# One decoder layer on one core: the sample maximum by way of TensorE, key sums one at a time, and low weights split on VectorE

## The reference

```python
z = x @ w_in                                  # q, k, v, u, two gates
s = einsum('bqhjd,bkhjd->bhjqk', q, k) * HEAD_DIM**-0.5 + bias   # 8 heads, two maps j
p = softmax(s); p_diff = p[:, :, 0] - lam * p[:, :, 1]
attn = rms_norm(einsum('bhqk,bkhe->bqhe', p_diff, v), subln_g) * (1 - lam_init)
ssm = g * sigmoid(g @ w_glu), g = gelu(s5_scan(u))               # 64 groups, 64 states
merged = sigmoid(gate_a) * (attn @ w_proj_attn) + sigmoid(gate_s) * (ssm @ w_proj_ssm)
h = layer_norm(alpha * x + merged @ w_out)
y = layer_norm(alpha * h + (silu(gate) * val) @ w_down)          # gate, val: conv(h @ w_up)
```

## Time and profile before

| | |
|---|---|
| runs, median | 1962.67 us (1961.89 to 1966.1, 3 runs) |
| profiled execution: time, span | 1960.97 us, 1959.1 us |
| mean granted clock of TensorE | 0.936 |
| PE matmul, busy | 1791.6 us (91%) |
| DVE, ACT, POOL busy | 1110.0, 604.7, 1116.0 us |
| DMA | 393.44 MB, 201 GB/s over the span |
| GpSimd line 620 (low weights), 166 instructions | 750.5 us |
| GpSimd line 583 (key products), 128 instructions | 299.2 us |
| VectorE line 1615 (key sums), 128 instructions | 153.9 us |

### The profile page before, as it was taken

How to read it: one execution, slowest core, us unless ns; L and a number is a source line. 1 busy time by engine, 2 the same in 40 slices (tenths; PEclk the granted TensorE clock), 3 DMA queues, 4 the chain that set the end, 5 groups by cost and what they waited for, 6 DMA issues and landing times.

```text
span 1959.1 us, 32040 instructions
## 1 busy us (share of the span) xinstructions
PE 1791.6 (91%) x11898; PEld 1530.8 (78%) x11898; DVE 1110.0 (57%) x1360; ACT 604.7 (31%) x927; POOL 1116.0 (57%) x383
## 2 busy tenths in 40 slices
PE   7899998898988969967999799999999997999997
PEld 5787665565655636646999799999999997999995
DVE  1353656556565563345950389999999999000004
ACT  2021222232222320212322354444444443333333
POOL 1036455465554643004777457777777777677771
PEclk9999898898988978978999989999999999999997
DMA  9766897888989866655656436666666665666651
GB/s 213 180 202 221 282 337 246 297 298 272 322 275 310 288 213 231 196 173 136 180 164 173 129 100 181 174 173 173 172 173 172 173 173 141 171 174 176 175 149 45
DMA packets 537197, 393.44 MB, mean 201 GB/s; under 512 B 23618, under 2 KB 502743, under 8 KB 536535
## 3 DMA queue, kind: packets, MB, share of 16 engines
q1 hardware_dynamic: 404944, 325.07, 55.4%
q10 hardware_dynamic: 132160, 67.11, 12.3%
HBM read 385.47 MB, written 7.02 MB: 200 GB/s over the span
## 4 chain that ended last, share of the span: by engine, by line
PE 55%; issue 14%; DMA 9%; DVE 9%; POOL 8%; SPq 3%; ACT 3%; DVEq 0%; ACTq 0%; POOLq 0%
PE bank L966 12%; PE bank L972 12%; PE bank L967 12%; PE bank L670 11%; DMA work<-in_cache_k 7%; POOL work L583 4%; POOL weights_lo L620 3%; PE bank L638 2%; DMA weight_ring<-in_w_in 2%; ACT weights_hi L1339 1%; PE bank L658 1%; DVE work L1615 1%; SPq L460 1%; SPq L398 1%; PE bank L751 1%
## 5 line engine op out<-in xcount | busy, mean ns | idle before, releaser
L620 POOL TENSOR_TENSOR weights_lo<-weight_ring,weights_hi 128x2048 fp32r<-128x2048 f32 (+1 forms) x166 | 750.5, 4532 | 371.6 <-ACT weights_hi L1339 208.8
L670 PE MATMUL bank<-work,weight_ring 128*128 128x264 f32 x2176 | 555.7, 411 | 7.8 <-DMA weight_ring<-in_w_in 7.3
L670 PEld LDWEIGHTS bank<-work,weight_ring 128*128 128x128 f32 x2176 | 425.1, 201 | 130.8 <-issue 56.7
L583 POOL TENSOR_TENSOR work<-work 128x1024 f32<-128x1024 f32 x128 | 299.2, 2352 | 212.0 <-DMA work<-in_cache_k 139.6
L1339 ACT ACTIVATE weights_hi<-weight_ring 128x2048 fp32r<-128x2048 f32 (+1 forms) x166 | 309.3, 1863 | 332.8 <-PE bank L967 315.6
L966 PE MATMUL bank<-h_hi,weights_hi 128*128 128x264 f32 x1376 | 345.1, 289 | 8.0 <-DVE h_lo L1811 8.0
L967 PE MATMUL bank<-h_lo,weights_hi 128*128 128x264 f32 x1376 | 340.7, 286 | 0.0
L966 PEld LDWEIGHTS bank<-h_hi,weights_hi 128*128 128x128 f32 x1376 | 260.7, 189 | 11.4 <-issue 8.4
L967 PEld LDWEIGHTS bank<-h_lo,weights_hi 128*128 128x128 f32 x1376 | 261.1, 190 | 0.0
L1615 DVE TENSOR_REDUCE work<-work 128x16 f32<-128x1024 f32 x128 | 153.9, 1216 | 165.8 <-POOL work L583 165.5
L972 PE MATMUL bank<-h_hi,weights_lo 128*128 128x264 f32 x1376 | 183.7, 286 | 5.6 <-POOL weights_lo L620 5.6
(11 more groups left out here) (233 smaller groups left out, 2192.0 us busy)
## 6 DMA issues: line engine op xcount, KB each, us to landing
weight_ring<-in_w_up SPq DMA_DIRECT2D x86, 1024.0 KB, 5.6
work<-in_cache_k SPq DMA_DIRECT2D x128, 512.0 KB, 6.0
work<-in_cache_v SPq DMA_DIRECT2D x128, 512.0 KB, 6.6
weight_ring<-in_w_in ACTq DMA_DIRECT2D x60, 1024.0 KB, 12.1
weight_ring<-in_w_down SPq DMA_DIRECT2D x32, 1024.0 KB, 5.9
weight_ring<-in_w_out SPq DMA_DIRECT2D x16, 1024.0 KB, 5.9
weight_ring<-in_w_down SPq DMA_DIRECT2D x16, 704.0 KB, 4.7
weight_ring<-in_w_proj_attn SPq DMA_DIRECT2D x16, 512.0 KB, 4.0
```

The source lines that it names most:

```text
L583: pool.tensor_tensor(page(k_pages, n), page(k_pages, n), q_b[b % 2], ALU.mult).then_inc(kq_ready, 1)
L620: pool.tensor_tensor(w_lo[:, cols].bitcast(F32R), slot3(off % SLOTS, 0, k_tiles).rearrange("p k m -> p (k m)"), w_hi[:, cols], ALU.subtrac ...
L670: last = pe.matmul(bank[n % 2][:, 0:N], slot(n % SLOTS, k), tiles[k], start=(k == 0), stop=(k == len(tiles) - 1))
```

## The change

The maximum over partitions leaves GpSimd: PE transposes the 16 columns of partition maxima into the mail bank (`max_rows`), VectorE reduces each of the 16 rows and multiplies the identity by the result (`all_max`), and PE's product of ones with that diagonal puts the 16 maxima on all partitions (`global_max`), from where `shift` reads them. On PE the users of the maximum stand later (the first page product in the third z tile instead of the second), and small products are put inside z tiles (`hooks`). `v_rows` is posted in the same head's first tile, `prompt_pv` at the start of the next head. A third score buffer lets VectorE run ahead. VectorE's key sums are placed one by one, some inside a scan step. SyncE's order is spelled out page by page. Beside that, `low`, the subtraction of the low weights, moves from GpSimd to VectorE: before `merge`, `residual`, the taps and the residual of w_down, for the tile one ahead. Gelu and copies on ScalarE are reordered to fit, and the mean squares stand behind glu tile 5 instead of 3.

```diff
-MAIL_ORDER = [("q_rows", 0), ("new_scores", 0), ("k_rows", 0), ("v_rows", 0)]
+MAIL_ORDER = [("q_rows", 0), ("new_scores", 0), ("k_rows", 0)]
 for _i in range(H):
-    MAIL_ORDER += [("combine", _i - 1)] if _i else []
-    MAIL_ORDER += [("sums", _i), ("p_diff", _i), ("attention", _i)]
-    MAIL_ORDER += [("k_rows", _i + 1), ("v_rows", _i + 1)] if _i + 1 < H else []
-MAIL_ORDER += [("kv_sample", 0), ("prompt_states", 0), ("sample_states", 0), ("combine", H - 1)]
+    MAIL_ORDER += [("attention", _i - 1)] if _i else []
+    MAIL_ORDER += [("v_rows", _i), ("max_rows", _i), ("max", _i)] + ([("combine", _i - 1)] if _i else [])
+    MAIL_ORDER += [("sums", _i), ("p_diff", _i)] + ([("k_rows", _i + 1)] if _i + 1 < H else [])
+MAIL_ORDER += [("attention", H - 1), ("kv_sample", 0), ("prompt_states", 0), ("sample_states", 0), ("combine", H - 1)]
...
+                for what in ("K4", "Sk", "P15", "V0", "K5", "V1", "K6", "Sv", "V2", "K7", "V3", "K8", "Q", "V4", "K9", "V5", "K10",
+                             "V6", "K11", "V7", "V8", "K12", "V9", "K13", "V10", "K14", "V11", "K15", "V12", "N0", "N1",
+                             "V13", "N2", "N3", "V14"):
...
-            def global_max(b):
-                pool.wait_ge(smax_ready, b + 1)
-                wait(pool, ssub_ready, b)
-                pool.partition_all_reduce(small[:, 528:544], small[:, 512:528], P,
-                                          bass.bass_isa.ReduceOp.max).then_inc(gmax_ready, 1)
...
-            def low(m, off, k_tiles):
-                pool.wait_ge(wh_ready, m + 1)
-                pool.wait_ge(slot_done, PROJ0 + m - 1)
-                cols = slice((off % 2) * KT * P, (off % 2) * KT * P + k_tiles * P)
-                pool.tensor_tensor(w_lo[:, cols].bitcast(F32R), slot3(off % SLOTS, 0, k_tiles).rearrange("p k m -> p (k m)"),
-                                   w_hi[:, cols], ALU.subtract).then_inc(wl_ready, 1)
...
+            def max_rows(b):
+                post(("max_rows", b))
+                pe.wait_ge(smax_ready, b + 1)
+                transpose(bank[2][0:16, 0:P], small[:, 512:528]).then_inc(mail, 1)
+
+            def global_max(b):
+                post(("max", b))
+                pe.wait_ge(gmax_ready, b + 1)
+                pe.matmul(bank[2][:, 0:16], ones[0:16, :], small[0:16, 528:544], start=True, stop=True).then_inc(mail, 1)
...
                 bu(t, 0)
                 bu(t, 1)
                 scores(i, 1, 0)
                 if i:
-                    z_tile(("v", i + 1), i - 1, (13, 14, 15))
-                else:
-                    z_tile(("v", i + 1))
+                    prompt_pv(i - 1)
+                z_tile(tiles[0], before(11, 12, 13) if whole else before(11, 12, 13, 14),
+                       {2: lambda: values_to_rows(i), 3: lambda: max_rows(i)})
                 scores(i, 1, 1)
-                if i + 2 < HT:
-                    z_tile(("u", i + 2), i, (0, 1))
+                z_tile(tiles[1], before(14, 15) if whole else before(15), {2: lambda: global_max(i)})
+                cx(t, 0)
+                bu(t, 2)
+                z_tile(tiles[2], now(0, 1, 2) if whole else now(0, 1, 2, 3), {2: lambda: scores(i, 0, 0)})
+                scores(i, 0, 1)
                 if i:
                     combine(i - 1)
                 denominators(i)
-                cx(t, 0)
-                bu(t, 2)
-                scores(i, 0, 0)
-                z_tile(("g", 4 * i), i, (2, 3, 4) if i + 2 < HT else (0, 1, 2, 3))
-                scores(i, 0, 1)
                 cx(t, 1)
                 bu(t, 3)
-                z_tile(("g", 4 * i + 1), i, (5, 6, 7) if i + 2 < HT else (4, 5, 6))
-                p_diff_rows(i)
+                z_tile(tiles[3], now(3, 4, 5) if whole else now(4, 5, 6, 7))
                 cx(t, 2)
-                if i == H - 2:
+                if not whole:
                     sample_bu()
-                z_tile(("g", 4 * i + 2), i, (8, 9, 10) if i + 2 < HT else (7, 8, 9))
-                prompt_pv(i)
+                z_tile(tiles[4], now(6, 7, 8) if whole else now(8, 9, 10, 11))
                 cx(t, 3)
-                keys_to_rows(i + 1)
-                z_tile(("g", 4 * i + 3), i, (11, 12) if i + 2 < HT else (10, 11, 12))
-                values_to_rows(i + 1)
-                if i == H - 2:
-                    sample_cx()
+                if whole:
+                    z_tile(tiles[5], now(9, 10), {1: lambda: p_diff_rows(i), 3: lambda: keys_to_rows(i + 1)})
...
+            p_diff_rows(H - 2)
+            keys_to_rows(H - 1)
+            prompt_pv(H - 2)
+            z_tile(("g", 28), [(B - 2, p) for p in (12, 13, 14)],
+                   {1: sample_cx, 2: lambda: values_to_rows(H - 1), 3: lambda: max_rows(B - 1)})
...
-                act.wait_ge(ssub_ready, b + 1)
-                act.activation(score[b % 2][:, 0:272], score[b % 2][:, 0:272], ACT.Exp).then_inc(sexp_ready, 1)
+                act.wait_ge(mail_read, MAIL["max", b] + 1)
+                act.activation(score[b % 3][:, 0:272], score[b % 3][:, 0:272], ACT.Exp).then_inc(sexp_ready, 1)
...
+                if between:
+                    between()
...
+            def all_max(b):
+                dve.wait_ge(mail, MAIL["max_rows", b] + 1)
+                wait(dve, mail, MAIL["max", b - 1] + 1 if b else 0)
+                dve.tensor_reduce(small[0:16, 544:545], bank[2][0:16, 0:P], AX.X, ALU.max).then_inc(mail_read, 1)
+                dve.wait_ge(mail_read, MAIL["max_rows", b] + 1)
+                dve.tensor_scalar(small[0:16, 528:544], ident[0:16, 0:16], small[0:16, 544:545], None, ALU.mult
+                                  ).then_inc(gmax_ready, 1)
+
             def shift(b):
-                dve.wait_ge(gmax_ready, b + 1)
-                s3 = score[b % 2][:, 0:272].rearrange("p (g c) -> p g c", c=16)
-                dve.tensor_tensor(s3, s3, small[:, 528:544].unsqueeze(1).to_broadcast([P, PAGES + 1, 16]),
-                                  ALU.subtract).then_inc(ssub_ready, 1)
+                dve.wait_ge(mail, MAIL["max", b] + 1)
+                s3 = score[b % 3][:, 0:272].rearrange("p (g c) -> p g c", c=16)
+                dve.tensor_tensor(s3, s3, bank[2][:, 0:16].unsqueeze(1).to_broadcast([P, PAGES + 1, 16]),
+                                  ALU.subtract).then_inc(mail_read, 1)
...
                 page_max(i)
-                states(t, 0)
-                shift(i)
-                reduce_pages(b, 0, 1)
-                states(t, 1)
+                states(t, 0, lambda: reduce_page(b, 0))
+                reduce_page(b, 1)
+                all_max(i)
+                states(t, 1, lambda: (shift(i), reduce_page(b, 2)))
+                maxima(i, 1)
+                reduce_page(b, 3)
                 page_sums(i)
-                maxima(i, 1)
-                reduce_pages(b, 2, 3, 4)
-                states(t, 2)
+                reduce_page(b, 4)
+                states(t, 2, lambda: reduce_page(b, 5))
+                reduce_page(b, 6)
                 maxima(i, 0)
-                reduce_pages(b, 5, 6, 7)
-                states(t, 3)
-                differences(i)
+                reduce_page(b, 7)
...
-                reduce_pages(b, 8, 9, 10, 11)
+                states(t, 3, lambda: reduce_page(b, 8))
+                reduce_page(b, 9)
+                differences(i)
+                reduce_page(b, 10)
                 map_weights(i)
-                y_out(t)
+                reduce_page(b, 11)
...
+            def low(m, off, k_tiles=KT):
+                dve.wait_ge(wh_ready, m + 1)
+                dve.wait_ge(slot_done, PROJ0 + m - 1)
+                cols = slice((off % 2) * KT * P, (off % 2) * KT * P + k_tiles * P)
+                dve.tensor_tensor(w_lo[:, cols].bitcast(F32R), slot3(off % SLOTS, 0, k_tiles).rearrange("p k m -> p (k m)"),
+                                  w_hi[:, cols], ALU.subtract).then_inc(wl_ready, 1)
+
             def merge(i):
                 for j in range(4):
                     n = 4 * i + j
+                    low(n + 1, j + 1)
...
+            low(0, 0)
             merge(0)
...
+                    low(KT + 4 * n + j + 1, j + 1)
                     residual(4 * n + j, j, PROJ + 4 * n + j + 1)
...
+                        low(SPLIT_UP + 4 * n + t + 1, t + 1)
                         dve.wait_ge(tap0, 4 * n + t + 1)
```

229 lines of the change are left out of this document (120 added, 109 removed).

## The result

The changed kernel took 1853.07 us in the median of four runs (1843.84 to 1866.63), against 1962.28 us for the one before (1959.99 to 1966.1); the ratio is 0.9447, with a 95% interval of 0.9371 to 0.9524. The forecast was 1850. The time came out right, but partly by luck: two of the steps that lead to it are wrong and offset each other. Ten runs of this kernel in all lie between 1832.1 and 1867.1 us; why they spread is part of the answer. The profiled execution is one of the slowest, 1866.63 us with a span of 1864.8, so its rows show the obstacle at its largest.

A forecast was written before the change was run, and what follows sets the result against it. GpSimd's maximum was taken to stall the seven heads, its low-weight subtraction four late places. Heads then set by DMA, -87; end of scan part +2; late part -26.4: 1961.0 becomes 1849.6, predicted 1850 us, range 1830 to 1892.

The forecast's parts named there:

- The maximum on GpSimd is what holds the heads.: Seven heads: the reduction costs GpSimd 17.2 us without a key product, delaying shift, exponential, page products and denominators.
- The rival by which the stream was held by DMA: Heads: DMA, not GpSimd, held the stream; heads stay at 82 us, 1937 us in all; chance 0.03.
- So I expect all three stalls to go.: Heads: PE waits before page products (32.3 us), denominators (31.0) and transposed probabilities (8.2) vanish, 71.6 us idle.
- DMA at 334 GB/s sets 71.9 us per full head.: Five full heads: 120 MB at 334 GB/s take 359 us; all seven heads 498 instead of 585, -87 us.
- by the rows at full DMA share: Heads: three stretches at DMA share 0.99 to 1.00 moved 325, 337 and 339 GB/s; their mean, 334, taken as DMA's rate.
- The second rival: Heads: PE sets all heads and nothing waits; 12 us less, 1838 us; chance 0.17.
- TensorE alone in 484 us: Seven heads on PE's work alone: 585 - 71.6 idle - 34 slow clock + 5 new instructions = 484 us (-101).
- The 358 GB/s: DMA in the heads: HBM limit per core from the Trainium skill; by it PE sets full heads, 10 to 12 us lower.
- I charge the queue nothing beyond the DMA rate.: Heads: SyncE's queue alternates key and value pages; cover of 12.5 us per page against 6.6 from issue to landing, no cost.
- the fourth rival: Heads: the maximum's five hand-overs close a cycle with the z tiles, PE waits in each head; 1988 us; chance 0.03.
- The end of the scan part, +2: Behind head 6: three mail posts with no tile between cost two hand-overs, +2 us; the 20.9 us value-page wait stays.
- The late part, -26.4: Subtraction on VectorE: first projection -7.8, w_out -4, 15 small waits -5.6, w_up to w_down -9 us.

The follow-up runs named there:

- reduce_gpsimd: The changed kernel with the maximum over partitions put back on GpSimd, between the key products of pages 1 and 2: 1922.4 us, ratio 0.9787.
- copy_first: The changed kernel, but in a head's third z tile ScalarE issues the weight load only after copying the combination and denominators out: 1827.4 us, ratio 0.9317.
- batched_sums: As copy_first, but VectorE's key sums in groups between whole scan steps, and the shift behind the second scan step: 1855.4 us, ratio 0.9468.
- queue_before: As copy_first, but SyncE's queue of pages has the order of the kernel before: 2016.9 us, ratio 1.0275.
- the two experiments: low_only and low_gpsimd, the move of the low-weight subtraction alone and left out: 1931.1 us and 1874.2 us.
- the second profile: Profile of a repeat of the changed kernel, unaltered: profiled run 1849.3 us, median of its six runs 1845.5 us.
- low_only: The kernel before with only the subtraction of the low weights moved from GpSimd to VectorE: 1931.1 us, ratio 0.9851.
- low_gpsimd: The changed kernel with the low weights subtracted on GpSimd again: 1874.2 us, ratio 0.9538.
- half_values: The changed kernel, loading only the first half of each value page's columns from the second sample on: 1822.5 us, ratio 0.9308.
- copy_first_params: As copy_first, with the convolution's parameters issued by GpSimd after its last key product instead of by SyncE: 1804.4 us, ratio 0.9222.

## Why the prediction was right in the time and wrong in two steps

- *The maximum on GpSimd is what holds the heads.* Right in that the reduction is the cause: with it back the heads are at 81 us and the time 76 us up (reduce_gpsimd). Of the chain that the forecast named (maximum, shift, exponential, page products) that run shows nothing, since the hole holds TensorE there by way of `rotation`; for the chain speak the rows of the kernel before and the 32.3 us of waiting that are gone. The rival by which the stream was held by DMA has fallen.
- *"So I expect all three stalls to go."* Two went. For the third I followed only the maximum, its shift and the sums, all early enough. I did not follow the mail: `denominators` may be posted when `combined` has been copied, and now both stand behind the same z tile, whose eviction ends with an issue. What was queued ahead of the copy on ScalarE was the thing to list. Cost: 27.3 us of waiting and some 20 of slow clock in the profiled run, 39 us between the two profiled spans (1864.8 and 1825.6), 19 us in the medians (copy_first against all ten runs).
- *DMA at 334 GB/s sets 71.9 us per full head.* Wrong: 66.8 us at 356 GB/s, set by TensorE. The failed step is "by the rows at full DMA share": in the three stretches of the earlier trace rows TensorE was busy for most of the time too, and a stretch in which both are busy doesn't tell which of the two is the limit. A share of 0.99 read as full was not: it went to 1.06 here. The second rival, TensorE setting all heads at 1838, was the better account of the limit: without the mail wait the kernel takes 1827, 11 us less still. Its term, TensorE alone in 484 us, was too large: copy_first runs the heads in 469.5 us, and about 5 of the 15 are work that now stands behind the boundary. One reason can be read in the kernel before. The forecast took all 71.6 us of waiting as time at half speed, but in head 3 the clock fell only in the course of the wait ahead of the page product (1.00 from 456.25 to 457, 0.50 from 459 on):

```profile
456.25:462.84 6.59, 0.00 (x0) 0.03 (x1) 1.00 (x2) 0.53 (x2) 0.39 (x1) 0.65 0.61 232
```

A mean clock of 0.65 while TensorE is idle leaves more of the slow time to its work than was reckoned.
- *The 358 GB/s.* The Trainium skill (HBM Reference, Specifications (TRN2)) gives about 358 GB/s as a core's share and says that a core which streams alone measures well above it; the 382 and 383 GB/s over 20 us, on one core with nothing beside it, agree with that, and the 358 that the prediction weighed as a limit was the figure for two cores at work.
- The two errors offset. Heads forecast at 498 us, measured 511 in this profile; head 0 and head 6 were 4 and 5 us shorter than forecast (64.2 and 65.7 against 68 and 71), the full ones 4.3 us longer each. That they leave the median within 3 us of the forecast is luck: without the mail wait the same 1850 would have stood against 1827 (copy_first).
- *"I charge the queue nothing beyond the DMA rate."* Right for the kernel as changed, by both edits together. Undone singly, they cost 28 us (batched_sums) and 190 us (queue_before). The last is the fourth rival's mechanism, a cycle that is closed, only through the key stream instead of the mail: there it gave 97 to 99 us per head where I had 91 ((484 + 7 x 21.7) / 7).
- *The end of the scan part, +2.* Mis-sized: 117.5 us instead of 108.6. 2.6 of the 8.9 is the wait at the value page, which stayed as forecast but grew to 23.5; 5.1 is TensorE's busy time (91.6 against 86.5), since the sample's state products (L848, 3.7 us) and others now stand behind the boundary and not ahead of it; head 6 is shorter by the same work.
- *The late part, -26.4.* Right: -29 and -28 by the medians of the two experiments, -31 and -20 by their profiles, -29.6 between the profiles of the two kernels. By pieces in the profiles: the first projection, from the last matmul of the scan part to the first product of low weights, 9.9 us instead of 17.3 (-7.4 against -7.8); w_out 93.9 instead of 96.5 us up to its first product of low weights and then no slow clock (-4 against -4); the rest, small waits and w_down, -18 against -14.6.
- By pieces the profiled run gives -74.2 (heads) + 8.9 (end of the scan part) - 29.6 (late part) + 0.5 (set-up) = -94.4, against -111.4 forecast; the median, 1853, is 14 us below this run, and the second profile, 17 us below it, has 17.5 us less of the mail wait.
- That VectorE's long instructions went with GpSimd's work is shown by low_only and low_gpsimd, which move the subtraction alone.

## What to carry to other kernels

A stretch in which an engine and the DMA are both busy gives a lower bound for each rate, not a limit; look for a stretch in which one of them waits. When a product is moved behind another on a shared buffer, list what stands ahead of the buffer's reader on its own engine, DMA issues among them, and give them their longest duration, not their median. When consumers move, the order in which the loads are issued has to move with them.

## What the runs showed of the hardware that was not expected

The issue of a 1 MB load by ScalarE took 0.4 us mostly and up to 8.22 us in heads where the DMA moved over 300 GB/s, and ScalarE did nothing of what stood behind it meanwhile; with 294 GB/s to move it stayed at 0.4 (half_values). The rate alone does not decide: in the heads of the kernel before no issue took over 0.46 us, through the stretches of 325 to 339 GB/s too, and in the set-up of the changed kernel one took 16.64 us while 58 GB/s were moved:

```profile
57.55 16.64 ACTq L331 DMA_DIRECT2D weight_ring<-in_w_in  x1
```

Why one issue is long and the next not, was not settled. On SyncE the same shows as an issue of 24.03 us for the convolution's weights behind the convolution's state, which is 86 x 16 pieces of 512 bytes; moved to GpSimd these issues cost TensorE nothing (copy_first_params).
